# Two-block transformer step on one core: block 1's gate steps and sigmoids a beat further apart, keys' decay ahead of the queries', pooled means in two beats, pooled products in a rotation bank

## The chip, the cores and the metric

One core of a Trainium2 chip runs the whole program. The metric is the device time of one execution in microseconds (us), the median of several; less is better. The engines are TensorE (PE, its weight loads PEld), VectorE (DVE), ScalarE (ACT), GpSimd (POOL) and SyncE (SP). Each runs its own list of instructions in order and waits on semaphores for the others.

## What is computed

512 tokens of 1024 features go through two blocks. Block 1, the one that is changed:

```python
h = rmsnorm(x, pre_norm_g)
q_a, f_a, i_a, g_a, u_b, g_b, q_c, k_c, v_c, g_c, f_c = split(h @ w_in)
# a: 4 heads of 64, gated recurrence
f_gate = lb + (1 - lb) * sigmoid(f_a);  log_f_a = log(max(f_gate, TINY))
k_a = (1 - lb) * sigmoid(-f_a)
o_a = hgrn2_chunkwise(silu(q_a), k_a, i_a, log_f_a)    # S_t = diag(f_t) S_{t-1} + k_t v_t^T, o_t = S_t^T q_t
o_a = rmsnorm(o_a per head) * silu(g_a)
# b: trailing means over 2, 4, 8, 16 tokens minus the token, a small product per group
o_b = (multiscale_pool(u_b) @ pool_w) * pool_scale * silu(g_b)
# c: 8 heads of 64, softmax(q k / 8 + sum of log forget), causal
o_c = forgetting_attention(q_c, k_c, v_c, log_sigmoid(f_c)) * silu(g_c)
x = x + rmsnorm(concat(o_a, o_b, o_c) @ w_out, post_norm_g)
```

Block 2 (window attention with sinks, latent attention, gates, a squared-ReLU feed-forward of width 4096) follows; the change does not touch it.

## The kernel before

Features lie on the 128 partitions and the 512 tokens along the free side. float32 products are made of three float32r products each: the high part of the weights by the high part of the features (L339), the high by the low (L340) and the low by the high (L341). A weight piece of 128x1024 is called a chunk. SyncE loads it, ACT rounds it to its high part (`hi`, L931), DVE subtracts to get the low part (`lo`, L1360), and PE uses it in 24 matmuls, six for each quarter.

Block 1's middle is written out by hand in 80 **beats** (`BEATS1`), and every engine walks through the same beats in one loop; a beat is only a place in each engine's order, not a time. What stands within a beat is done in the order of the code. The table `FILL1` gives each beat one or two quarters of a chunk for PE, so that PE always has large products between the small ones. Around them run:

- **Attention, 16 steps n of 4 beats.** PE: scores at beat 4n (L545), transposes of the weights (`turn`, L556) at 4n+5, product with the values (`weighted`, L572) at 4n+8. DVE: maxima (L1452) at 4n, the division (L1467, L1471) at 4n+3. ACT: exponents (L1090) at 4n. The transposed weights are copied out of their two banks at beat 4n+6, one by ACT (L1100) and one by DVE (L1478); `weighted` at 4n+8 waits for both.
- **Gate steps of the two head pairs p = 0, 1**, counted from the beat in which the chunk with f_a ends (beats 2 and 30): DVE L1616 (`gz`), ACT three functions (`ga1`, L1125 to L1129), DVE two (`gb`, L1621, L1622), ACT two (`ga2`, L1132, L1134), DVE four (`gf`, `gc`, `kh`, L1625 to L1631), ACT two (`ga3`, L1137, L1139), DVE two with the scan (`gs`, `bh`, L1634, L1636).
- **Sigmoid products (silu) of ten tiles** from the table `SILU1`: DVE L1602, L1606 at `start`, ACT three functions (L1177 to L1181) at `start` + 1, DVE the product (L1609) at the end.
- **The recurrence of pair p from beat `REC[p]`** (10 and 40): for eight levels DVE takes differences (L1575), ACT two exponents (L1112, L1113), POOL two products (L1988, L1993), PE a product of 16 small matmuls (L597, beats REC+3 to REC+10), and DVE merges it by a mask (L1564) one beat later. All levels use the banks 6 and 7, so a level waits for the merge of the one before. Then DVE L1643, ACT L1150 (queries' decay) and L1152 (keys' decay), POOL L1997 (queries) and L1999 (keys), PE transposes the keys (L606), makes states (L617), outputs (L629, L633) and head sums (L640).
- **The pooled part**: POOL window sums (L2010), DVE means (L1694, L1697), PE the product (L650) at `POOLED` (beats 51 and 62), ACT its scaling (L1166), which frees its bank.

The banks 2, 4 and 5 are taken in turn by the chunks (`turns`).

Of the kernel before, what the change touches and what calls it, by code (L numbers as in the profile page):

```python
# [82 lines left out]
for c in range(CH["w1e", 0], CH["w1e", 9] + 1):  # L83
    for quarter in range(4):
# [6 lines left out]
SILU1_AT = [END1[CH[SILU1_OF[s][0], SILU1_OF[s][1] * p + SILU1_OF[s][2]]] + 1 for s, p in SILU1]  # L91
SILU1_END = {s: t + 2 for s, t in zip(SILU1, SILU1_AT)}

REC = [max(END1[CH["w1e", 2 * p]] + 7, SILU1_END["q", p]) + 1 for p in range(2)]
POOLED = [next(t for t in range(END1[CH["w1e", 4 + 2 * p]] + 6 + 2 * p, BEATS1)
               if all(t - r < 3 or t - r == 11 or t - r > 17 for r in REC)) for p in range(2)]

# [67 lines left out]
def build(nc, A, out):  # L165
    with ExitStack() as ctx:
# [167 lines left out]
        def pe(e):  # L334
# [306 lines left out]

            def pooled(p):
                bank, before = tenant(6 + p, "pw", p)
                if before:
                    e.wait_ge(*to(*before))
                e.wait_ge(*to("wp", p, 1))
                if p == 0:
                    for g in range(4):
                        e.wait_ge(semaphore(f"pw{g}"), 16)
                e.matmul(bank[:], PWM[:, p, :], WP, start=True, stop=True).then_inc(*up("pm", p))  # L650
# [14 lines left out]
            for t in range(BEATS1):  # L665
# [6 lines left out]
                for p in range(2):  # L672
                    d = t - REC[p]
                    if 3 <= d < 11:
                        level(p, d - 3)
                    if d == 12:
                        keys_by_token(p)
                    if d == 13:
                        states(p)
                    if d == 15:  # L680
                        outputs(p)
                    if d == 16:
                        head_sums(p)
                    if t == POOLED[p]:
                        pooled(p)
                for c, q in FILL1.get(t, ()):
# [238 lines left out]
        def act(e):  # L925
# [177 lines left out]
            for t in range(BEATS1):  # L1103
# [15 lines left out]
                for p in range(2):  # L1119
# [3 lines left out]
                    if d == 2:  # L1123
# [5 lines left out]
                        e.activation(x, x, ACT.Ln, bias=one).then_inc(*up("ga1", p, 2))  # L1129
                    if d == 4:  # L1130
                        e.wait_ge(*to("gb", p, 0))
                        e.activation(BH, BH, ACT.Exp).then_inc(*up("ga2", p, 0))  # L1132
                        e.wait_ge(*to("gb", p, 1))
                        e.activation(KH, x, ACT.Exp, scale=-1.0).then_inc(*up("ga2", p, 1))  # L1134
                    if d == 6:
                        e.wait_ge(*to("gc", p, 0))
# [9 lines left out]

                    d = t - REC[p]
                    if d == 10:
                        e.wait_ge(*to("bh", p))
                        e.activation(QE, BH, ACT.Exp).then_inc(*up("qx", p))  # L1150
                        e.wait_ge(*to("ux", p))
                        e.activation(UR[1], UR[1], ACT.Exp).then_inc(*up("uy", p))  # L1152
                        e.activation(eb, BH[:, 127:T:128], ACT.Exp).then_inc(*up("eb", p))
# [200 lines left out]
        def dve(e):  # L1354
# [184 lines left out]
            for t in range(BEATS1):  # L1539
# [57 lines left out]
                for k, ((s, p), start) in enumerate(zip(SILU1, SILU1_AT)):  # L1597
                    z, o = ZS[k % 2], silu_out(s, p)
                    if t == start:
# [6 lines left out]
                        e.tensor_scalar(o, z, ZMIN, None, ALU.max).then_inc(*up("sm", s, p))  # L1606
                    if t == start + 2:
                        e.wait_ge(*to("sa", s, p, 2))
                        e.tensor_tensor(o, o, z, ALU.mult).then_inc(*up("silu", s, p))  # L1609
                for p in range(2):  # L1610
# [3 lines left out]
                    if d == 1:  # L1614
                        e.wait_ge(*to("gemm", CH["w1e", 2 * p]))
                        e.tensor_tensor(z, seat["gz", p][:], R[:], ALU.mult).then_inc(*up("gz", p))  # L1616
                    if d == 3:
                        if p:
# [3 lines left out]
                        e.scalar_tensor_tensor(x, z, 0.0, x, ALU.max, ALU.add).then_inc(*up("gb", p, 1))  # L1622
                    if d == 5:
                        e.wait_ge(*to("ga2", p, 0))
# [6 lines left out]
                        e.tensor_scalar(KH, KH, oml[:, p:p + 1], None, ALU.mult).then_inc(*up("kh", p))  # L1631
                    if d == 7:
                        e.wait_ge(*to("ga3", p, 1))
# [5 lines left out]
                    d = t - REC[p]  # L1639
                    if d == 10:  # L1640
                        b3, U = (x_.rearrange("p (c s) -> p c s", c=4) for x_ in (BH, UR[1]))
# [43 lines left out]
                    if t == a + 1:  # L1685
                        e.wait_ge(*to("gemm", CH["w1e", 4 + 2 * p]))
                        e.wait_ge(*to("zero", 5))
                        e.tensor_tensor(U[:, 16:528], seat["pu", p][:], R[:], ALU.mult).then_inc(*up("pu", p))
                    if t == a + 4:
                        for b in range(2):  # L1690
                            s = (V, UP2)[b]
# [255 lines left out]
        def pool(e):  # L1947
# [31 lines left out]
            for t in range(BEATS1):  # L1979
                for p in range(2):  # L1980
                    d = t - REC[p]
                    for lv in range(7):
                        if d == (lv if lv > 1 else 0):
# [9 lines left out]
                            e.tensor_tensor(U[:, :, 0:m], U[:, :, 0:m], k[:, :, 0:m],  # L1993
                                            ALU.mult).then_inc(*up("u2", p, lv))
                    if d == 10:
                        e.wait_ge(*to("qx", p))
                        e.tensor_tensor(QE, QE, QH, ALU.mult).then_inc(*up("qe", p))  # L1997
                        e.wait_ge(*to("uy", p))
                        e.tensor_tensor(UR[1], UR[1], KH, ALU.mult).then_inc(*up("ut", p))  # L1999
                    if t == END1[CH["w1e", 4 + 2 * p]] + 1:  # L2000
# [243 lines left out]
```

## Time and profile before

| what | us |
|---|---|
| runs of the kernel before | 1004.94, 1009.93, 1005.14 (median 1005.14) |
| the profiled execution: own time, span | 1009.88, 1008.6 |
| PE busy, PEld busy | 969.3, 790.3 |
| DVE, ACT, POOL busy | 592.7, 425.7, 103.6 |

The span is from the first to the last instruction. A busy PE need not run at its full rate: matmuls overlap, and the clock that the chip grants it is listed apart. In a timeline a row gives the start, the duration, the engine and line, what is written and read, and in brackets how long the engine was idle just before and what ended that. Where the text speaks of a beat's time, it is the start of the first row that belongs to it.

### The profile page before, as it was taken

The numbers are of one execution on the slowest core, as the hardware profiler recorded it, in microseconds if no ns is written. First come the engines' busy times: TensorE is split into PE (matmuls) and PEld (weight loads), VectorE is DVE, ScalarE is ACT, GpSimd is POOL, SyncE is SP. The second block draws the span as 40 slices with busy tenths as digits, with TensorE's granted clock in tenths as the row PEclk, the third lists the DMA queues.
The fourth block names the chain that finished last, engine by engine and source line by source line (L and its number), as shares of the span: only waits on it lengthen the run. The fifth ranks groups of instructions, "written<-read, shape, count | busy, mean of one in ns | idle before, by whom it ended". The sixth has DMA issues, their size and how long they took to land.

```text
span 1008.6 us, 13904 instructions
## 1 busy us (share of the span) xinstructions
PE 969.3 (96%) x5344; PEld 790.3 (78%) x5344; DVE 592.7 (59%) x1104; ACT 425.7 (42%) x816; POOL 103.6 (10%) x110
## 2 busy tenths in 40 slices
PE   9999999999999998999998999999999999999996
PEld 8868777767898775766776889888888888888895
DVE  6467559758748676656655751784235335434456
ACT  6354246345555244645544323463233224213331
POOL 2004103310030000000000312021000000000020
PEclk9999999999999999999999999999999999999999
DMA  7221122112223311212222252253322332332102
GB/s 248 82 83 48 38 64 83 43 42 77 95 92 122 129 42 50 72 30 71 63 63 62 86 188 84 77 215 105 98 91 84 105 97 92 104 105 84 42 1 84
DMA packets 25809, 86.74 MB, mean 86 GB/s; under 512 B 2960, under 2 KB 5712, under 8 KB 25488
## 3 DMA queue, kind: packets, MB, share of 16 engines
q1 hardware_dynamic: 23952, 80.25, 25.0%
q10 hardware_dynamic: 1552, 5.28, 1.4%
q8 instruction: 43, 0.70, 0.3%
q0 software_dynamic: 240, 0.33, 0.1%
q14 instruction: 22, 0.18, 0.1%
HBM read 81.65 MB, written 4.19 MB: 85 GB/s over the span
## 4 chain that ended last, share of the span: by engine, by line
PE 81%; DVE 11%; ACT 5%; issue 3%; POOL 0%; DVEq 0%; ACTq 0%
PE PB L339 11%; PE PB L341 11%; PE PB L340 11%; PE PB L900 5%; PE PB L901 5%; PE PB L899 5%; PE PB L545 3%; PE PB L572 3%; DVE wl L1360 2%; PE PB L556 2%; PE PB L865 1%; PE PB L370 1%; PE PB L867 1%; PE PB L371 1%; PE PB L375 1%
## 5 line engine op out<-in xcount | busy, mean ns | idle before, releaser
L339 PE MATMUL PB<-hh,wh 128*128 128x512 f32 x592 | 248.1, 419 | 3.5 <-DVE AR L1779 1.9
L341 PE MATMUL PB<-hh,wl 128*128 128x512 f32 x592 | 232.5, 393 | 0.0
L340 PE MATMUL PB<-hl,wh 128*128 128x512 f32 x592 | 231.9, 392 | 0.0
L1360 DVE TENSOR_TENSOR wl<-raw,wh 128x1024 fp32r<-128x1024 f32 (+2 forms) x92 | 117.4, 1276 | 65.0 <-ACT wh L931 64.9
L339 PEld LDWEIGHTS PB<-hh,wh 128*128 128x128 f32 x592 | 111.8, 189 | 36.2 <-issue 12.2
L341 PEld LDWEIGHTS PB<-hh,wl 128*128 128x128 f32 x592 | 111.5, 188 | 24.5
L340 PEld LDWEIGHTS PB<-hl,wh 128*128 128x128 f32 x592 | 112.1, 189 | 23.8 <-issue 3.3
L931 ACT ACTIVATE wh<-raw 128x1024 fp32r<-128x1024 f32 (+2 forms) x92 | 93.5, 1019 | 55.8 <-PE PB L867 13.7
L1090 ACT ACTIVATE S<-S,sm 128x256 f32<-128x256 f32 (+3 forms) x96 | 50.8, 530 | 129.0 <-DVE sm L1452 92.2
L1360 DVE TENSOR_TENSOR wl<-AR,wh 128x1024 fp32r<-128x1024 f32 x55 | 67.7, 1231 | 46.0 <-ACT wh L931 46.0
L931 ACT ACTIVATE wh<-AR 128x1024 fp32r<-128x1024 f32 x55 | 57.9, 1052 | 70.3 <-PE PB L901 70.3
L899 PE MATMUL PB<-gh,wh 128*128 128x512 f32 x224 | 87.1, 389 | 0.0
L900 PE MATMUL PB<-gl,wh 128*128 128x512 f32 x224 | 87.1, 389 | 0.0
L901 PE MATMUL PB<-gh,wl 128*128 128x512 f32 x224 | 87.1, 389 | 0.0
L1896 DVE TENSOR_TENSOR tmp<-tmp 128x512 f32<-128x512 f32 x32 | 23.2, 726 | 77.1 <-ACT gh L1306 77.1
L1302 ACT ACTIVATE tmp<-PB 128x512 f32<-128x512 f32 x32 | 19.1, 596 | 90.0 <-PE PB L341 87.8
L1452 DVE CUSTOM_DVE_ANT_0 S<-PB,MK 128x128 f32<-128x128 f32 (+3 forms) x64 | 29.9, 490 | 37.9 <-PE PB L545 37.1
L899 PEld LDWEIGHTS PB<-gh,wh 128*128 128x128 f32 x224 | 42.0, 188 | 8.8
L900 PEld LDWEIGHTS PB<-gl,wh 128*128 128x128 f32 x224 | 42.0, 188 | 8.7
L901 PEld LDWEIGHTS PB<-gh,wl 128*128 128x128 f32 x224 | 42.0, 188 | 8.7
L1961 POOL TENSOR_TENSOR acc<-acc,tmp 128x512 f32<-128x512 f32 x11 | 15.9, 1450 | 315.2 <-ACT tmp L1330 284.6
L572 PE MATMUL PB<-PT,AR 128*64 128x128 f32 x432 | 34.7, 286 | 11.2 <-ACT PT L1100 5.7
(356 smaller groups left out, 1722.5 us busy)
## 6 DMA issues: line engine op xcount, KB each, us to landing
AR<-in_dne SPq DMA_DIRECT2D x32, 512.0 KB, 3.5
AR<-in_upe SPq DMA_DIRECT2D x24, 512.0 KB, 3.5
raw<-in_w2g SPq DMA_DIRECT2D x16, 512.0 KB, 3.5
raw<-in_w1e SPq DMA_DIRECT2D x10, 512.0 KB, 3.5
raw<-in_w1q SPq DMA_DIRECT2D x8, 512.0 KB, 3.4
raw<-in_woab SPq DMA_DIRECT2D x8, 512.0 KB, 3.5
raw<-in_w2e SPq DMA_DIRECT2D x6, 512.0 KB, 4.1
X<-in_xT SPq DMA_DIRECT2D x4, 512.0 KB, 6.4
```

The costliest lines, as they stand in the source:

```text
L339: e.matmul(bank[:], a[:, col(k)], xa[:, k, :], start=k == 0, stop=False)
L340: e.matmul(bank[:], a[:, col(k)], xb[:, k, :], start=False, stop=False)
L341: i = e.matmul(bank[:], b[:, col(k)], xa[:, k, :], start=False, stop=k == 7)
L545: last = e.matmul(bank[b][:, k], query[b], key[b][:, k], start=a == 2, stop=x == parts - 1)
L572: x = e.matmul(bank[rows(b), col(i)], v, PT[b][:, j - lo, :], start=j == lo, stop=j == i)
L899: e.matmul(bank[:], a[:, col(k)], gh[:, k, :], start=k == 0, stop=False)
L900: e.matmul(bank[:], a[:, col(k)], gl[:, k, :], start=False, stop=False)
L901: i = e.matmul(bank[:], b[:, col(k)], gh[:, k, :], start=False, stop=k == 7)
L931: e.activation(wide_high if c == LAST else wh[c % 3][:, 0:PLAN[c][2]], raw_of(c), ACT.Copy).then_inc(*up("hi", c))
L1090: e.activation(s, s, ACT.Exp, bias=nm, scale=-1.0, accum_out=su).then_inc(*up("exp", a, n, b))
L1360: e.tensor_tensor(low_, raw_of(c), high.bitcast(F32), ALU.subtract).then_inc(*up("lo", c))
L1452: e.tensor_tensor_reduce(soft(n, b)[:, 0:w], seat["max", a, n, b][:, 0:w], MK[:, T - w:T], -1.0, BIG, ALU.add, ALU.min, scalars(n, b)[0]). ...
```

## The change

Six tables and places are edited:

- A silu takes 3 beats instead of 2 from its start to the DVE product; the ACT part stays in beat `start` + 1.
- Gate steps, in beats after the chunk's end: `gb` 3 to 4, `ga2` 4 to 5, `gf`/`gc`/`kh` 5 to 7, `ga3` 6 to 8, `gs`/`bh` 7 to 10. `gz` and `ga1` stay at 1 and 2.
- `REC` goes from (10, 40) to (13, 41).
- L1643 and the keys' decay (ACT L1152, POOL L1999) go to REC + 9, the queries' stay at REC + 10. They were all at REC + 10, queries first.
- The second half of each pooled mean goes one beat later.
- `POOLED` stays (51, 62), by a shorter rule; its product takes the next of the banks 2, 4, 5 instead of bank 6 or 7.

```diff
-SILU1_END = {s: t + 2 for s, t in zip(SILU1, SILU1_AT)}
-
-REC = [max(END1[CH["w1e", 2 * p]] + 7, SILU1_END["q", p]) + 1 for p in range(2)]
-POOLED = [next(t for t in range(END1[CH["w1e", 4 + 2 * p]] + 6 + 2 * p, BEATS1)
-               if all(t - r < 3 or t - r == 11 or t - r > 17 for r in REC)) for p in range(2)]
+SILU1_END = {s: t + 3 for s, t in zip(SILU1, SILU1_AT)}
+
+REC = [max(END1[CH["w1e", 2 * p]] + 10, SILU1_END["q", p]) + 1 for p in range(2)]
+POOLED = [END1[CH["w1e", 4 + 2 * p]] + 6 + 2 * p for p in range(2)]
...
-            def pooled(p):
-                bank, before = tenant(6 + p, "pw", p)
-                if before:
-                    e.wait_ge(*to(*before))
+            def pooled(p, at):
+                bank, before = tenant(at, "pw", p)
+                e.wait_ge(*to(*before))
...
-                        pooled(p)
+                        pooled(p, (2, 4, 5)[turns % 3])
+                        turns += 1
...
-                    if d == 4:
+                    if d == 5:
                         e.wait_ge(*to("gb", p, 0))
...
-                    if d == 6:
+                    if d == 8:
                         e.wait_ge(*to("gc", p, 0))
...
                     d = t - REC[p]
+                    if d == 9:
+                        e.wait_ge(*to("ux", p))
+                        e.activation(UR[1], UR[1], ACT.Exp).then_inc(*up("uy", p))
                     if d == 10:
                         e.wait_ge(*to("bh", p))
                         e.activation(QE, BH, ACT.Exp).then_inc(*up("qx", p))
-                        e.wait_ge(*to("ux", p))
-                        e.activation(UR[1], UR[1], ACT.Exp).then_inc(*up("uy", p))
...
-                    if t == start + 2:
+                    if t == start + 3:
                         e.wait_ge(*to("sa", s, p, 2))
...
-                    if d == 3:
+                    if d == 4:
                         if p:
                             e.wait_ge(*to("ho", 0))
...
-                    if d == 5:
+                    if d == 7:
                         e.wait_ge(*to("ga2", p, 0))
...
-                    if d == 7:
+                    if d == 10:
                         e.wait_ge(*to("ga3", p, 1))
...
-                    if d == 10:
+                    if d == 9:
                         b3, U = (x_.rearrange("p (c s) -> p c s", c=4) for x_ in (BH, UR[1]))
...
-                    if t == a + 4:
-                        for b in range(2):
+                    for b in range(2):
+                        if t == a + 4 + b:
...
+                    if d == 9:
+                        e.wait_ge(*to("uy", p))
+                        e.tensor_tensor(UR[1], UR[1], KH, ALU.mult).then_inc(*up("ut", p))
                     if d == 10:
                         e.wait_ge(*to("qx", p))
                         e.tensor_tensor(QE, QE, QH, ALU.mult).then_inc(*up("qe", p))
-                        e.wait_ge(*to("uy", p))
-                        e.tensor_tensor(UR[1], UR[1], KH, ALU.mult).then_inc(*up("ut", p))
```

VectorE, the first pair's gate, beats 5 to 6, before (L1621 and L1622 are `gb`, L1360 the low part of a chunk, L1478 a softmax copy, L1602 and L1606 the start of a silu):

```order
L1621 SCALAR_TENSOR_TENSOR AR<-early 128x512
L1622 SCALAR_TENSOR_TENSOR early<-early 128x512
L1360 TENSOR_TENSOR wl<-raw,wh 128x1024
L1478 COPY PT<-PB 128x128
L1602 TENSOR_TENSOR tmp<-PB,R 128x512
L1606 TENSOR_SCALAR AR<-tmp 128x512
```

and in the changed kernel:

```order
L1360 TENSOR_TENSOR wl<-raw,wh 128x1024
L1478 COPY PT<-PB 128x128
L1602 TENSOR_TENSOR tmp<-PB,R 128x512
L1606 TENSOR_SCALAR AR<-tmp 128x512
L1621 SCALAR_TENSOR_TENSOR AR<-early 128x512
L1622 SCALAR_TENSOR_TENSOR early<-early 128x512
```

The two steps `gb` stand behind four others now. Pair 1 has the same exchange in beats 33 and 34.

VectorE, the second pair, beats 33 to 35, before (L1467 and L1471 divide the softmax, L1625 to L1631 are `gf`, `gc` and `kh`):

```order
L1621 SCALAR_TENSOR_TENSOR AR<-early 128x512
L1622 SCALAR_TENSOR_TENSOR early<-early 128x512
L1360 TENSOR_TENSOR wl<-raw,wh 128x1024
L1478 COPY PT<-PB 128x512
L1602 TENSOR_TENSOR tmp<-PB,R 128x512
L1606 TENSOR_SCALAR AR<-tmp 128x512
L1467 RECIPROCAL sm<-sm 128x2
L1471 TENSOR_SCALAR S<-S,sm 128x128 x2
L1625 TENSOR_SCALAR AR<-AR,sm 128x512
L1628 TENSOR_SCALAR early<-AR 128x512
L1630 TENSOR_SCALAR early<-AR 128x512
L1631 TENSOR_SCALAR AR<-AR,sm 128x512
```

and where L1625 to L1631 stand in the changed kernel, beats 36 and 37 (L1452 are the maxima, L1609 a silu's product):

```order
L1452 ISA S,sm<-PB,MK 128x256
L1452 ISA sm 128x1
L1452 ISA S,sm<-PB,MK 128x256
L1452 ISA sm 128x1
L1360 TENSOR_TENSOR wl<-raw,wh 128x1024
L1609 TENSOR_TENSOR AR<-AR,tmp 128x512
L1602 TENSOR_TENSOR tmp<-PB,R 128x512
L1606 TENSOR_SCALAR AR<-tmp 128x512
L1625 TENSOR_SCALAR AR<-AR,sm 128x512
L1628 TENSOR_SCALAR early<-AR 128x512
L1630 TENSOR_SCALAR early<-AR 128x512
L1631 TENSOR_SCALAR AR<-AR,sm 128x512
```

The four steps went from ahead of the maxima to behind the maxima, the next chunk's low part and two pieces of silu.

ScalarE, beats 36 to 38, before (L1137 and L1139 are `ga3`, L1031 rounds an attention output, L1177 to L1181 a silu, L1100 the softmax copy of step 8):

```order
L1090 ACTIVATE S,sm<-S,sm 128x256 x2
L931 ACTIVATE wh<-raw 128x1024
L1137 ACTIVATE early<-early 128x512
L1139 ACTIVATE early<-early 128x512
L1031 ACTIVATE gh<-tmp 128x512
L1177 ACTIVATE AR<-AR 128x512
L1179 ACTIVATE AR<-AR,con 128x512
L1181 ACTIVATE AR<-AR 128x512
L1100 ACTIVATE PT<-PB 128x128
```

and in the changed kernel, where these lines have numbers that are one lower:

```order
L1089 ACTIVATE S,sm<-S,sm 128x256 x2
L930 ACTIVATE wh<-raw 128x1024
L1136 ACTIVATE early<-early 128x512
L1138 ACTIVATE early<-early 128x512
L1177 ACTIVATE AR<-AR 128x512
L1179 ACTIVATE AR<-AR,con 128x512
L1181 ACTIVATE AR<-AR 128x512
L1030 ACTIVATE gh<-tmp 128x512
L1099 ACTIVATE PT<-PB 128x128
```

On this engine only the rounding of the attention output moved here; the same instructions stand ahead of the softmax copy.

## Rows read from the trace of the kernel before

**Rows 1.** The page: busy time of PE, and the chain that ended last by engine

```profile
PE 969.3 (96%) x5344; PEld 790.3 (78%) x5344; DVE 592.7 (59%) x1104; ACT 425.7 (42%) x816; POOL 103.6 (10%) x110
...
PE 81%; DVE 11%; ACT 5%; issue 3%; POOL 0%; DVEq 0%; ACTq 0%
```

**Rows 2.** Waits of PE, 51 to 252 us: total, times, longest

```profile
PE PB L597 <- DVE AR L1564: 3.6, 3, 2.3
PE PB L572 <- ACT PT L1100: 2.3, 1, 2.3
PE PB L606 <- ACT early L1166: 2.2, 1, 2.2
PE PB L606 <- POOL AR L1999: 1.9, 1, 1.9
PE PB L572 <- DVE PT L1478: 0.7, 1, 0.7
```

**Rows 3.** Busy time by 5 us stretches; behind "PEclk" is the granted clock

```profile
75.00:80.00 5.00, 4.54 (x23) 3.17 (x24) 3.30 (x6) 2.37 (x6) 3.96 (x6) 0.66 0.01 3
115.00:120.00 5.00, 5.00 (x27) 3.64 (x27) 2.63 (x8) 0.00 (x0) 0.00 (x0) 0.66 0.04 16
195.00:200.00 5.00, 2.72 (x21) 2.14 (x20) 4.36 (x9) 1.41 (x4) 0.73 (x1) 0.82 0.15 56
200.00:205.00 5.00, 5.00 (x18) 3.72 (x17) 1.64 (x5) 2.63 (x4) 0.55 (x1) 0.84 0.00 0
```

**Rows 4.** Timeline of PE: beats 12 and 40, and the keys' transposes of pair 1

```profile
75.47 1.12 PE L572 MATMUL PB<-PT,AR 128*64 128x128 f32 x8 [2.34 <-ACT PT L1100]
...
161.41 0.44 PE L572 MATMUL PB<-PT,AR 128*64 128x128 f32 x4
...
209.45 0.55 PE L606 MATMUL PB<-con,AR 128*128 128x128 f32 x3 [2.22 <-ACT early L1166]
```

**Rows 5.** Timeline of ACT ahead of beat 12

```profile
60.38 1.04 ACT L931 ACTIVATE wh<-raw 128x1024 fp32r<-128x1024 f32 x1
...
73.81 0.42 ACT L1112 ACTIVATE AR<-AR 128x256 f32<-128x256 f32 x1 [3.43 <-DVE AR L1575]
...
75.05 0.36 ACT L1100 ACTIVATE PT<-PB 128x256 f32<-128x256 f32 x1
```

**Rows 6.** Timeline of DVE, beats 33 to 38

```profile
147.75 0.69 DVE L1621 SCALAR_TENSOR_TENSOR AR<-early 128x512 f32<-128x512 f32 x1 [2.75 <-ACT early L1129]
...
148.96 1.22 DVE L1360 TENSOR_TENSOR wl<-raw,wh 128x1024 fp32r<-128x1024 f32 x1
...
151.76 0.16 DVE L1467 RECIPROCAL sm<-sm 128x2 f32<-128x2 f32 x1
...
152.35 0.54 DVE L1625 TENSOR_SCALAR AR<-AR,sm 128x512 f32<-128x512 f32 x1
...
156.72 1.23 DVE L1360 TENSOR_TENSOR wl<-raw,wh 128x1024 fp32r<-128x1024 f32 x1 [0.37 <-ACT wh L931]
157.87 0.68 DVE L1602 TENSOR_TENSOR tmp<-PB,R 128x512 f32<-128x512 f32 x1
...
158.93 0.68 DVE L1634 TENSOR_TENSOR early<-early 128x512 f32<-128x512 f32 x1
```

**Rows 7.** Timeline of ACT, beats 33 to 38

```profile
147.56 1.04 ACT L931 ACTIVATE wh<-raw 128x1024 fp32r<-128x1024 f32 x1
...
155.65 1.04 ACT L931 ACTIVATE wh<-raw 128x1024 fp32r<-128x1024 f32 x1
156.60 0.61 ACT L1137 ACTIVATE early<-early 128x512 f32<-128x512 f32 x1
...
157.64 0.61 ACT L1031 ACTIVATE gh<-tmp 128x512 fp32r<-128x512 f32 x1
159.05 0.64 ACT L1177 ACTIVATE AR<-AR 128x512 f32<-128x512 f32 x1 [0.80 <-DVE AR L1606]
...
161.01 0.26 ACT L1100 ACTIVATE PT<-PB 128x128 f32<-128x128 f32 x1
```

## The prediction

> **What bounds the kernel now.** I read the page first: PE is busy for 969.3 us of 1008.6, and the chain that ended last is PE for 81% [rows 1]. No other engine is near that, so only two things can be won: stretches in which PE stands idle, and stretches in which it runs below its full clock. The change touches block 1 alone, which lies between 51 and 252 us. The waits of PE there sum up to 10.7 us in seven places [rows 2]. In order of time they are: 2.34 us at beat 12 (the first L572 behind the softmax copy of step 1 [rows 4]), 0.80 before a level, 1.89 before the keys' transposes of pair 0, 0.52 and 2.28 before levels of pair 1, 2.22 before pair 1's keys' transposes [rows 4], and 0.69 before L572 at beat 60. The clock view adds a second price. It shows four stretches of 5 us below 1.00: 0.66, 0.66, 0.82 and 0.84 [rows 3]. They are three falls to the lower of the two levels, 1.2 instead of 2.4 GHz, and stand behind the waits of 2.34, 1.89 and 2.28 us. Each loses 5 x 0.34 = 1.7 us (the third 5 x 0.18 + 5 x 0.16 = 1.7), 5.1 us in all. The wait of 2.22 us had no such fall behind it. So block 1 holds 15.8 us that can be won in the profiled execution.
>
> The profiled execution took 1009.88 us, the median of the three runs is 1005.14, and one run took 1009.93. The difference of 4.7 is about the 5.1 us of the three falls. I take 1005.1 to be an execution without them, which no row proves. Half a per cent, 5 us, is about what a measurement of this kernel can tell from no change.
>
> **What the change removes.** Wait by wait:
> - The keys' transposes of pair 0 waited for POOL L1999, which stood behind the queries' L1997 in the beat just before. Now the keys' product starts three beats ahead of the transposes. Between them PE has two levels and some 24 large matmuls, an estimate of over 6 us, and the chain is one instruction each of DVE, ACT and POOL (L1643, L1152, L1999), so the 1.89 us go. The queries' product is needed three beats after the keys', so turning the two round costs nothing.
> - The transposes of pair 1 waited 2.22 us for L1166, since the pooled product sat in their bank 6. In a rotation bank it blocks the third chunk after it, six or more beats later. The 2.22 us go. Pooled product 1 shifts the last chunk to bank 5, which the output projection wants seventh; DVE L1602 frees it about then, which costs 0.1 us at most.
> - The 2.28 us before a level of pair 1 waited for a merge (L1564) behind both halves of the pooled mean, four instructions of together 1.9 us. Half of these now stand a beat later, still a beat ahead of the pooled product that reads them, and the levels stand a beat later too. By the sum of DVE's instructions in the two beats the merge is ready when PE comes. The 0.52 and 0.80 us before levels go likewise: the levels of pair 0 begin three beats after the gates, not beside them.
> - The 0.69 us at beat 60 go, because the head norm now comes behind that copy.
> - Beat 12 keeps most of its wait. The softmax copy stood behind pair 0's exponents [rows 5]; these move to beat 13, but the gate steps come closer. I lay the durations out from L931's end at 61.42 [rows 5]: low part, copy and silu start take 2.4 us on DVE, `gb` 1.3 (65.1); ACT does `ga2`, three sigmoid steps, exponents and the next high part until 69.9; DVE follows with low part, two products and four gate steps, 4.0 us, and ACT ends `ga3` and the copy at 74.7. PE could start at 74.8 instead of 75.47 [rows 4], so 0.67 us are won.
> That is 0.80 + 1.89 + 0.52 + 2.28 + 2.22 + 0.69 + 0.67 = 9.1 us of idle time.
>
> **What the change adds.** The same thing happens to pair 1, where before there was no wait: PE took L572 of beat 40 at 161.41 without one [rows 4], ACT's copy having begun at 161.01 [rows 7]. Laid out step by step:
> 1. `gb` stands behind the low part. DVE must now wait for L931, which ends at 147.56 + 1.04 = 148.60 [rows 7]. Low part, copy, L1602 and L1606 took 151.76 - 148.96 = 2.8 us [rows 6], so `gb` runs from 151.4 to 152.7 instead of 147.75 to 149.0 [rows 6].
> 2. ACT: `ga2` until 153.3, three sigmoid steps 2.0, two exponents 1.0, high part 1.04, until 157.3 (before 156.69 [rows 7]).
> 3. DVE: low part 1.15 (156.72 to 157.87 [rows 6]), L1609 0.6, L1602 and L1606 1.06 (157.87 to 158.93 [rows 6]), then L1625 and L1628 1.0. `gc` is ready at 161.1. Before, L1625 began at 152.35 [rows 6] and ACT could start `ga3` at 156.60 [rows 7].
> 4. ACT: `ga3` 1.1, three sigmoid steps and the copy 2.2 (159.05 to 161.27 [rows 7]), the rounding L1031 0.5: the copy ends at 165.0. PE wanted it at 161.41.
> This makes a wait of 3.6 us. Pair 0's head norm, now in beats 29 and 30, pushes `gz` by an estimated 0.9 us more (its four dependent DVE steps stand ahead of the division and of `gz`), so the bounds are 3.6 and 4.5 and I take 4.1. Queued behind that copy are ACT's next high part and exponents, and behind PE's L572 all of PE.
> Next late is pair 1's scan at beat 40, then the first exponents and the copy for beat 44: 0.85 us if PE runs at full clock, nothing if it is slowed. Beat 16 has the like for pair 0, 0.55 or nothing. Pair 1's states at beat 54 wait for a DVE copy that now stands behind L1712 and a silu product: 1.0 us. Together 5.1 us if PE is slowed, 6.5 if not. The later silu products cost nothing by themselves: their readers (the attention output L1712, the levels, the pooled and recurrent outputs) were put at or behind the new beat, and PE's large products of that beat cover them. No DMA is moved: SyncE's queue is as before, and its loads follow the low parts, whose place among the beats is the same; the one low part that is later, by 0.6 us in step 3, is read three beats on.
>
> **The clock.** The three falls of before go with their waits, but new waits stay at beats 12 (1.7 us) and 40 (4.1 us), and I take both to have a fall behind them, 3.4 us. The bounds are none and six. *The Trainium skill* ("TensorE: Matmul & The Clock Gate", Part 1) has the gate look at activity at times that do not follow the kernel's start, so that the same kernel can fall in one run and not in another. By that rule the runs of before at 1005 and 1010 would differ in this alone, and the change would move the slower kind more than the faster. The trace has a wait of 2.28 us with a fall and one of 2.22 without [rows 2, 3], which fits it; the sum does not need it.
>
> **The sum.** Against the profiled execution: 1009.9 - 9.1 + 5.1 - 5.1 + 3.4 = 1004.2. Against 1005.1 taken as free of falls: 1005.1 - 9.1 + 5.1 + 3.4 = 1004.5, or without any fall 1005.1 - 9.1 + 6.5 = 1002.5. I predict 1004.0.
>
> **The rivals.**
> - *The knot at beat 38 is not there.* If `gc` is ready before ACT comes to it, ACT's copy is in time and 4.1 + 1.7 us fall away: 998.2. For it: the instructions ahead of the copy are the same as before. Against it: `gc` is ready 7.8 us later by the sums above (161.1 against 152.35 + 1.0 [rows 6]); before, even the last gate step L1634 had begun by 158.93 [rows 6].
> - *Waits only move.* DVE is what PE waits for behind both levels [rows 2], so each us won before a level might come back one beat later. All in all no time is won: 1005.1. For it: the 0.80 and 0.52 us. Against it: the two waits at the transposes have other causes.
> - *Slower: the clock falls behind the small waits too.* At full clock the new waits are 6.5 us, which gives 1002.5. Each fall adds 1.7. From five falls on, behind the waits at beats 12, 16, 40, 44 and 54, it is 1011.0, slower than before by over half a per cent; four make 1009.3. For it: 1.89 us sufficed once. Against it: the waits of 0.52 to 0.80 us had no fall, nor had the one of 2.22 us [rows 2, 3].
>
> **How the numbers follow.** The forecast has a chance of 0.50, the absent knot 0.22, the moved waits 0.16, the clock 0.12. Faster by over half a per cent (below 1000.1): 0.22 and a tail of 0.05 of the forecast's, 0.27. Slower (above 1010.2): 0.12. Within: 0.61. The range goes from 998.5, next to the absent knot, to 1009.5, just short of the fifth fall.
>
> **What would show it.** In the trace after, PE waits at beat 40 for ACT's copy (L1099) for 3.6 to 4.5 us, and ACT ahead of it for `gc` (L1136 behind DVE's L1628). PE waits 1.7 us at beat 12 for a copy. Neither transposes (L605) nor levels (L596) have waits over 0.5 us. A wait at beat 40 under 1 us, or a new one over 2 us elsewhere in block 1, would make the prediction wrong, as would falls of the clock that do not follow waits.

## The result and the profile after

The kernel before took 1006.63 us (median of five runs, 1004.94 to 1009.93), the changed one 1014.71 (five runs, 1014.05 to 1015.71). The ratio is 1.0074 with a 95% interval of [1.0047, 1.01]: slower by 0.74%. (Here and below the ratio is worked out from all runs; it is not the quotient of the two medians.) Predicted were 1004.0 us and a range of 998.5 to 1009.5.

The profiled execution of the changed kernel took 1014.05 us. Its page, which answers to [rows 1]:

```profile
span 1012.8 us, 13904 instructions
...
PE 969.6 (96%) x5344; PEld 791.4 (78%) x5344; DVE 592.9 (59%) x1104; ACT 425.0 (42%) x816; POOL 104.4 (10%) x110
...
PE 75%; DVE 13%; ACT 7%; issue 3%; POOL 0%; DVEq 0%; ACTq 0%
```

PE is as busy as before, within 0.3 us, in a span that is 4.2 us longer: the time went into idleness of PE. In the chain that ended last, PE has 75% instead of 81%. The waits of PE in block 1 (51 to 252 us), as in [rows 2]. Most line numbers are one lower than before: L571 is `weighted`, L596 a level, L616 the states, L1099 the ACT copy.

```profile
PE PB L571 <- ACT PT L1099: 6.7, 4, 4.1
PE PB L596 <- POOL AR L1988: 2.2, 1, 2.2
PE PB L616 <- issue: 1.3, 1, 1.3
PE PB L596 <- DVE AR L1564: 1.1, 2, 0.8
...
```

The same view of 252 to 290 us, behind the beats. In the kernel before it has no row at all.

```profile
PE PB L338 <- DVE wl L1360: 2.3, 1, 2.3
PE PB L369 <- DVE tmp L1602: 0.7, 1, 0.7
```

The two stretches sum up to 14.5 us of idle time (before: 10.7). In the timeline of PE the four that matter most are:

```profile
91.20 1.11 PE L596 MATMUL PB<-AR 64*128 64x64 f32 x16 [2.17 <-POOL AR L1988]
...
163.57 0.44 PE L571 MATMUL PB<-PT,AR 128*64 128x128 f32 x4 [4.10 <-ACT PT L1099]
...
252.01 0.50 PE L369 MATMUL PB<-gh,wh 128*128 128x512 f32 x1 [0.67 <-DVE tmp L1602]
...
275.06 0.50 PE L338 MATMUL PB<-gh,wh 128*128 128x512 f32 x1 [2.33 <-DVE wl L1360]
```

The granted clock in stretches of 5 us, the answer to [rows 3] (the third number from the end):

```profile
90.00:95.00 5.00, 3.80 (x29) 3.76 (x30) 3.10 (x10) 4.94 (x13) 2.71 (x4) 0.74 0.01 3
95.00:100.00 5.00, 5.00 (x47) 4.76 (x46) 3.73 (x6) 1.96 (x5) 3.06 (x3) 0.92 0.30 105
160.00:165.00 5.00, 1.43 (x12) 1.29 (x14) 2.58 (x8) 4.35 (x8) 0.00 (x0) 0.91 0.03 8
165.00:170.00 5.00, 5.00 (x21) 3.82 (x18) 4.13 (x9) 1.31 (x4) 0.00 (x0) 0.75 0.17 47
...
550.00:555.00 5.00, 5.00 (x27) 4.12 (x28) 1.40 (x2) 2.18 (x3) 0.00 (x0) 0.68 0.01 3
```

Three falls, each of about 1.7 us (5 x 0.26 + 5 x 0.08, and so on): behind the waits of 2.17 and 4.10 us, and one in block 2, where the change moves nothing.

### The profile page after: what moved, and what is told of

Same layout as the page of the kernel before. It is cut to its first block, busy times and chain, and to the rows that moved or that the text cites. A ratio compares the mean times of both kernels' runs of the same rounds, so it can differ in the third digit from the quotient of the medians.

```text
span 1012.8 us, 13904 instructions
## 1 busy us (share of the span) xinstructions
PE 969.6 (96%) x5344; PEld 791.4 (78%) x5344; DVE 592.9 (59%) x1104; ACT 425.0 (42%) x816; POOL 104.4 (10%) x110
## 4 chain that ended last, share of the span: by engine, by line
PE 75%; DVE 13%; ACT 7%; issue 3%; POOL 0%; DVEq 0%; ACTq 0%
PE PB L338 10%; PE PB L340 10%; PE PB L339 10%; PE PB L900 5%; PE PB L899 5%; PE PB L898 5%; PE PB L544 3%; DVE wl L1360 3%; PE PB L571 3%; ACT wh L930 2%; PE PB L864 1%; ACT S L1089 1%; PE PB L865 1%; PE PB L866 1%; PE PB L555 1%
## 5 line engine op out<-in xcount | busy, mean ns | idle before, releaser
L1360 DVE TENSOR_TENSOR wl<-raw,wh 128x1024 fp32r<-128x1024 f32 (+2 forms) x92 | 117.7, 1280 | 84.0 <-ACT wh L930 83.8
L338 PEld LDWEIGHTS PB<-hh,wh 128*128 128x128 f32 x592 | 111.5, 188 | 35.8 <-issue 11.7
L1360 DVE TENSOR_TENSOR wl<-AR,wh 128x1024 fp32r<-128x1024 f32 x55 | 67.7, 1231 | 46.0 <-ACT wh L930 46.0
L1452 DVE CUSTOM_DVE_ANT_0 S<-PB,MK 128x128 f32<-128x128 f32 (+3 forms) x64 | 29.9, 489 | 33.9 <-PE PB L544 33.1
L571 PE MATMUL PB<-PT,AR 128*64 128x128 f32 x432 | 35.1, 289 | 14.9 <-ACT PT L1099 10.1
L571 PEld LDWEIGHTS PB<-PT,AR 128*64 128x64 f32 x432 | 23.5, 139 | 32.1 <-issue 18.6
```

The source lines that it names most:

```text
L338: e.matmul(bank[:], a[:, col(k)], xa[:, k, :], start=k == 0, stop=False)
L571: x = e.matmul(bank[rows(b), col(i)], v, PT[b][:, j - lo, :], start=j == lo, stop=j == i)
L1360: e.tensor_tensor(low_, raw_of(c), high.bitcast(F32), ALU.subtract).then_inc(*up("lo", c))
L1452: e.tensor_tensor_reduce(soft(n, b)[:, 0:w], seat["max", a, n, b][:, 0:w], MK[:, T - w:T], -1.0, BIG, ALU.add, ALU.min, scalars(n, b)[0]). ...
```

## One reading for all runs

Each run lists its span and its mean granted clock. A run's time multiplied by that clock is what it would have taken without the falls; I call it the clock-free time. Runs of one kernel that lie up to 8 us apart agree in it within 3 us (the clock is listed to 0.001, which is 1 us). It comes out some 2.4 to 2.8 us too low for every kernel, since the clock also falls over about the last 5 us of the program, when PE has nothing to do (granted clock 0.50 from 1004 us on before, from 1008 us on after). Beside it stands what the profile shows as PE's waits from 51 to 290 us, summed up. The medians and ratios are those of the runs below, each beside runs of the kernel before in the same round; "rest" is clock-free time less waits.

| kernel | runs | median us | ratio to before | clock-free us | waits us | rest |
|---|---|---|---|---|---|---|
| before | 5 to 35 | 1006.6 to 1009.6 | | 1002.0 | 10.7 | 991.3 |
| after | 5 | 1014.71 | 1.0074 [1.0047, 1.01] | 1005.6 | 14.5 | 991.1 |
| e8, after again | 6 | 1016.18 | 1.0068 [1.0044, 1.0091] | 1005.5 | 14.5 | 991.0 |
| e1, `ga` silu back | 12 | 1010.04 | 1.0018 [1.0001, 1.0034] | 1003.4 | 11.2 | 992.2 |
| e2, pair 1's gates back | 12 | 1009.38 | 1.0007 [0.9991, 1.0022] | 1003.5 | 11.7 | 991.8 |
| e9, all silus back | 12 | 1008.09 | 0.9993 [0.9972, 1.0014] | 999.6 | 8.6 | 991.0 |
| e3, bank alone | 12 | 1011.76 | 1.0013 [0.999, 1.0036] | 1000.6 | 9.5 | 991.1 |
| e4, keys alone | 12 | 1006.32 | 0.9983 [0.9965, 1.0] | 1000.2 | 9.0 | 991.2 |
| e5, means alone | 12 | 1008.61 | 1.0006 [0.9989, 1.0024] | 1000.9 | 9.6 | 991.3 |
| e6, silus alone | 11 | 1011.95 | 1.0042 [1.0025, 1.0059] | 1004.1 | 12.3 | 991.8 |
| e7, bank, keys, means | 12 | 1004.51 | 0.9965 [0.9949, 0.9981] | 998.4 | 7.5 | 990.9 |
| e10, e7 and `REC` 11, 40 | 6 | 1002.63 | 0.9934 [0.9912, 0.9955] | 996.7 | 5.8 | 990.9 |
| e11, e10 and an early copy | 6 | 999.10 | 0.9898 [0.9876, 0.9919] | 995.5 | 4.0 | 991.5 |

The rest is 990.9 to 992.2 for all of them, while the waits go from 4.0 to 14.5. So, within about 1 us, a microsecond in which PE waits here costs a microsecond, and what is left of a difference between medians is the clock. Nothing is given back later: behind 290 us PE's waits sum up to 17.3 us before and 17.2 after, in the same places. For the changed kernel: 3.8 us more of waits, and a median 9.1 us above its clock-free time where before's first five runs stood 4.6 above theirs.

## The experiments

The expectations reckon from 1006.6 us, the first five runs of the kernel before. In the rounds of the experiments the same kernel had medians of 1009.54 (e1 to e4), 1009.64 (e5 to e7) and 1008.06 (e8 to e11), so their absolute times are up to 3 us low from the start. What decides is the wait that each expects, and the clock-free time.

**e1: is the tail the `ga` silus?** The sigmoid products of `ga`, the last of which falls behind the beats' end, go back to `start` + 2.

```diff
-SILU1_END = {s: t + 3 for s, t in zip(SILU1, SILU1_AT)}
+SILU1_END = {s: t + (2 if s[0] == "ga" else 3) for s, t in zip(SILU1, SILU1_AT)}
...
-                    if t == start + 3:
+                    if t == SILU1_END[s, p]:
```

> The changed kernel with the two last silu tiles (ga, pairs 0 and 1) back at their old distance of 2 beats. Tail theory: the loss behind the beats comes from the DVE products and roundings of these tiles, which push the angle chain and with it the low part for which the output projection waits (2.33 us, and 0.7 for bank 5); the wait before the fifth chunk of the projection goes, the time falls by about 3 us from 1014.7 to 1011.6. Knot theory (the loss is in the waits at beats 12, 16, 17 and 40): no change, 1014.7 within 0.5. Clock theory (the loss is how often the clock falls): the wait goes, but the time moves by whole falls of 1.7 us in either direction.

Measured: median 1010.04. Between 252 and 290 us the waits are gone, and the rows of the tail stand where they stood in the kernel before, to 0.01 us:

```profile
258.23 0.42 DVE L1722 CAST S<-AR 128x512 f32<-128x512 int32 x1
...
270.95 1.22 DVE L1360 TENSOR_TENSOR wl<-raw,wh 128x1024 fp32r<-128x1024 f32 x1 [4.10 <-ACT wh L930]
```

It follows that 3.0 us of waits came from these two entries of the table. The wait of 4.10 stayed (4.12). PE's waits fell by 3.3 us in all, the clock-free time by only 2.2; about 1 us between this kernel's waits and its time is not accounted for.

**e2: is the knot at beat 40 the gates?** Pair 1's gate steps go back to their old offsets, pair 0's stay.

```diff
-                    if d == 5:
+                    if d == (5, 4)[p]:
...
-                    if d == 8:
+                    if d == (8, 6)[p]:
...
-                    if d == 4:
+                    if d == (4, 3)[p]:
...
-                    if d == 7:
+                    if d == (7, 5)[p]:
...
-                    if d == 10:
+                    if d == (10, 7)[p]:
```

> The changed kernel with the gate steps of pair 1 alone back at their old offsets (REC of pair 1 stays 41). Knot theory: the wait of 4.1 us at beat 40 goes and with it a fall of the clock, 1014.7 - 4.1 - 1.7 = 1008.9. Tail theory: the tail is not touched, its 3 us stay, so 1009 is also the floor here. If the wait at beat 40 were made by the shifted attention output or by pair 0's head norm instead, at least 3 us of it would stay and the time would be above 1012.

Measured: 1009.38. Of the 4.10 us, 1.91 remained, so pair 1's gates are 2.2 of them and not the whole; it was expected to go. The tail kept its 0.67 and 2.33, as it should.

**e3: the rotation bank alone**, on the kernel before.

```diff
-                        pooled(p)
+                        pooled(p, (2, 4, 5)[turns % 3])
+                        turns += 1
```

> The kernel before with only the pooled products in the rotation banks. The wait of 2.22 us before pair 1's key transposes goes; nothing else moves: 1006.6 - 2.2 = 1004.4. Rival: the last chunk of the beats now sits in bank 5 and the output projection waits for it (0.7 to 1.1 us), which leaves 1005.3 or so. If waits only move, 1006.6.

Measured: 1011.76, ratio 1.0013. The wait of 2.22 us is gone, but the states L617 (L616 after) come with 1.7 us that were not there. PE reaches them sooner, and the copy of the transposed keys on DVE (L1649), queued behind a low part and the start of a silu, is not ready (e11 tests this). The 0.69 us at beat 60 went too, so the net gain is 1.2 us (10.7 to 9.5). Bank 5 made no wait. That this kernel's median is no better is the clock: seven of its twelve runs lie at 1011.7 to 1013.6 with a mean clock of 0.987 or 0.989, the other five at 1005.3 to 1007.5 with 0.994 or 0.996.

**e4 and e5: the keys' decay alone, the means alone**, on the kernel before.

```diff
-                    if d == 10:
+                    if d == 9:
                         b3, U = (x_.rearrange("p (c s) -> p c s", c=4) for x_ in (BH, UR[1]))
```

```diff
-                    if t == a + 4:
-                        for b in range(2):
+                    for b in range(2):
+                        if t == a + 4 + b:
```

(In e4 the keys' exponent on ACT and their product on POOL go to 9 with it, as in the change.)

> The kernel before with only the keys' decay a beat earlier and ahead of the queries'. The wait of 1.89 us before pair 0's key transposes goes, and the fall of the clock behind it: 1006.6 - 1.9 - 1.7 = 1003.0; without the fall 1004.7. Rival: the DVE difference and the ACT exponent now come before ACT's copy of the softmax in that stretch and one of these is late: 1006.6 or more.

> The kernel before with only the second half of each pooled mean a beat later. The four DVE instructions ahead of the merge that PE waits for (2.28 us in the trace before, beat 50) become two; the merge is about 1 us earlier if its beat holds the second half behind it: the wait shrinks to 1.3 us or less, and the clock may not fall: 1006.6 - 1.0 = 1005.6, with the fall 1003.9. If waits only move: 1006.6.

Measured: 1006.32 and 1008.61. In e4 the wait of 1.89 us for POOL is gone and a level waits 0.2 longer, so 1.7 is won. In e5 the level's 2.28 shrinks to 1.17: the mean was half of it. For the rest, the rows show DVE at other work in those beats; no run tried it.

**e6: the silus alone**, on the kernel before. Since pair 1's queries end a beat later, `REC` becomes (10, 41).

```diff
-SILU1_END = {s: t + 2 for s, t in zip(SILU1, SILU1_AT)}
+SILU1_END = {s: t + 3 for s, t in zip(SILU1, SILU1_AT)}
...
-                    if t == start + 2:
+                    if t == start + 3:
```

> The kernel before with only the silu products a beat later (this moves REC of pair 1 to 41 too, since its query silu ends later). Tail theory: the low part for the projection is 2.85 us later here too and PE waits for it about 2.3 us: 1006.6 + 2.3 = 1008.9 or more. Knot theory: no wait over 1 us appears at the tail, 1006.6.

Measured: 1011.95, slower than before by 0.42%, from this edit and the one beat of `REC` that comes with it. PE's waits, with the tail's:

```profile
PE PB L572 <- ACT PT L1100: 4.4, 2, 2.9
PE PB L597 <- DVE AR L1564: 2.7, 2, 1.9
...
PE PB L339 <- DVE wl L1360: 2.7, 1, 2.7
```

The first row counts two waits. The second of them is 1.50 us at beat 40, where before had none: the silus begin the knot with the old gates. In the rows there, ACT's rounding of the attention output (L1031) waits 0.39 us for its DVE product (L1712), which now stands behind the scan, and the softmax copy stands behind that rounding. The last row is the tail.

**e9: the silus back**, on the changed kernel: the reverse of e6's edit. `REC` stays (13, 41).

> The changed kernel with all silu products back at 2 beats; gates, REC (13, 41) and the three moves as changed. Tail theory: the whole tail wait (2.33 and 0.7) goes. Knot theory as put in the prediction (the gate steps alone make the wait at beat 40): about 3.5 us of the 4.1 stay, floor 1009.0 - 3.1 - 0.5 = 1005.4. If silu and gates make that wait together, 2 us or less of it stay: floor 1003.8 or less.

Measured: 1008.09, ratio 0.9993. No wait behind 252 us, and in block 1:

```profile
PE PB L571 <- ACT PT L1099: 4.7, 3, 3.0
PE PB L596 <- POOL AR L1988: 2.2, 1, 2.2
...
```

The gates without the silus make 3.0 us at beat 40, the silus without the gates 1.5, both 4.1. Neither expectation (3.5 stays, or 2 and less) was met; the two share the wait. The clock-free time fell from 1005.6 to 999.6.

**e7: the three moves without gates and silus**: e3, e4 and e5 together, on the kernel before.

> The kernel before with the three moves that cost nothing in the trace after: rotation bank, keys' decay first, pooled mean in two beats. Gates, silu and REC as before. If the single gains add up: 2.2 + 1.9 + 1.0 of waits and up to two falls of 1.7: 1006.6 - 5.1 - 3.4 = 998.1; without the falls 1001.5. If waits only move, 1005 or more.

Measured: 1004.51, ratio 0.9965 [0.9949, 0.9981], the first kernel that is faster. Its waits:

```profile
PE PB L597 <- DVE AR L1565: 2.8, 3, 1.4
PE PB L572 <- ACT PT L1100: 2.3, 1, 2.3
PE PB L617 <- issue: 1.7, 1, 1.7
...
```

**e8: the changed kernel again**, beside e9 to e11.

> The changed kernel, unchanged, beside the others. Floor theory: a run takes a floor that is fixed by the waits, plus 1.4 to 1.7 us for every fall of the clock. The floor of this kernel is 1014.05 - 5.1 = 1009.0 by its trace, that of before 1009.9 - 5.1 = 1004.8; the runs should lie on 1009.0, 1010.6, 1012.2, 1013.9, 1015.5 and before on 1004.8 to 1012.5 in the same steps. Rival: the spread is noise without steps, and the ratio stays at 1.0074.

Measured: 1016.18, ratio 1.0068 [1.0044, 1.0091], with the same waits. The profiled execution took 1017.50 and had five falls: those of the three places above, one at 275 behind the tail's 2.33, and one at 345 to 355 in block 2. Of the expected ladder (1009.0, 1010.6, 1012.2, 1013.9, 1015.5) the lower half was not seen: all eleven runs of this kernel, in both rounds, lie between 1014.05 and 1017.5, so a changed kernel without falls is worked out and not measured.

**e10 and e11: on from e7.** e10 puts pair 0's recurrence one beat later, beside the old gates; e11 also moves DVE's copy of the transposed keys ahead of the low part of its beat (and takes it out of its old place, which the cut leaves out).

```diff
-REC = [max(END1[CH["w1e", 2 * p]] + 7, SILU1_END["q", p]) + 1 for p in range(2)]
+REC = [max(END1[CH["w1e", 2 * p]] + 8 - p, SILU1_END["q", p]) + 1 for p in range(2)]
```

```diff
+                for p in range(2):
+                    d = t - REC[p]
+                    if d == 12:
+                        e.wait_ge(*to("kp", p))
+                        if p:
+                            e.wait_ge(*to("sg", 0))
+                        e.tensor_copy(KT, seat["kt", p][:, 0:384].rearrange("p (c s) -> p c s", c=3)).then_inc(
+                            *up("kt", p))
                 for c, end in END1.items():
                     if t == end + 1:
                         lo(c + 2)
```

> The three moves (rotation bank, keys first, mean in two beats) on the kernel before, with the recurrence of pair 0 one beat later (REC 11 instead of 10), gates and silu as before. The softmax copies of step 1 then stand ahead of pair 0's first differences and exponents on DVE and ACT: the wait at beat 12 shrinks from 2.34 to 0.5 us and no clock fall follows. Floor 1000.2 - 1.8 = 998.4. If waits only move, the levels of pair 0 wait instead and the floor stays at 1000.2.

> As the run before, and the DVE copy of the transposed keys stands ahead of the low part and the silu steps of its beat. The wait of pair 1's states (1.7 us with the three moves) was put down to nothing in the profile; if it is this copy, it goes and the floor falls by 1.2 to 1.7 us more. If it is something else, the time does not change.

Measured: 1002.63 and 999.10. In e10 the 2.34 us at beat 12 shrink to 0.40 with one beat for `REC[0]` and no gate step moved. In e11 the 1.7 us ahead of the states are gone too. What is left of PE's waits in block 1 in e11:

```profile
PE PB L597 <- DVE AR L1565: 3.1, 3, 1.4
PE PB L572 <- DVE PT L1479: 0.9, 2, 0.5
```

e11 is faster than before by 1.0% (0.9898 [0.9876, 0.9919]) and its median is 17 us below that of the changed kernel in the same round (e8). From e10 to e11 the waits fell by 1.8 us and the clock-free time by 1.2; the rest of the 3.5 us between the medians is the clock.

## Why the prediction was wrong, by its own steps

**The knot at beat 40 was right in its chain, and met its number in part by luck.** Predicted was a wait of 3.6 to 4.5 us for ACT's copy with `gc` (L1628) late ahead of it, taken at 4.1. The timeline of ACT and DVE there (compare [rows 6, 7]):

```profile
155.86 1.23 DVE L1360 TENSOR_TENSOR wl<-raw,wh 128x1024 fp32r<-128x1024 f32 x1 [2.91 <-ACT wh L930]
157.00 0.68 DVE L1609 TENSOR_TENSOR AR<-AR,tmp 128x512 f32<-128x512 f32 x1
...
158.67 0.54 DVE L1625 TENSOR_SCALAR AR<-AR,sm 128x512 f32<-128x512 f32 x1
159.24 0.43 DVE L1628 TENSOR_SCALAR early<-AR 128x512 f32<-128x512 f32 x1
...
159.71 0.63 ACT L1136 ACTIVATE early<-early 128x512 f32<-128x512 f32 x1 [3.88 <-DVE early L1628]
...
162.70 0.61 ACT L1030 ACTIVATE gh<-tmp 128x512 fp32r<-128x512 f32 x1
163.22 0.26 ACT L1099 ACTIVATE PT<-PB 128x128 f32<-128x128 f32 x1
```

ACT sits 3.88 us until `gc` is there, does `ga3`, three sigmoid steps and a rounding, and comes to the copy at 163.22; PE starts at 163.57. The copy ends 1.5 us earlier than in the prediction (163.5 against 165.0), and PE wants it 1.9 us earlier (159.47 against 161.41). The two misses nearly cancel, and a wait of 4.10 is the 3.6 of the sum with that difference, not with the head norm's 0.9 that the prediction had added by estimate. Of its parts the rounding L1030 and the product L1609 (0.5 and 0.6 us) come from the silus: without them it was 3.0 (e9).

**So were the small ones.** Beat 12: 1.66 us (predicted 1.7). Beat 16: 0.64 (0.55 or 0). Beat 44: 0.33 (0.85 or 0). States at beat 54: 1.26 (1.0). The waits at the transposes and those of 0.52 and 0.69 us went, as said. Block 1's last beat ended 0.9 us earlier than before, in spite of 0.7 us more idle time within it: one fall fewer lay there.

**Failed: "The later silu products cost nothing by themselves."** The step looked at who reads the products and at PE's work in the beats, and the prediction took its waits from 51 to 252 us alone, as "the change touches block 1 alone". It did not lay out what the products do to DVE's and ACT's queues in the last beats and behind them, where DVE and ACT already work out the sines for the next block's positions (the angle chain, L1722 to L1738). The timeline after:

```profile
250.67 0.68 DVE L1609 TENSOR_TENSOR early<-early,tmp 128x512 f32<-128x512 f32 x1
...
253.06 0.63 ACT L1030 ACTIVATE gh<-AR 128x512 fp32r<-128x512 f32 x1 [3.56 <-DVE AR L1678]
253.59 0.62 ACT L1177 ACTIVATE early<-early 128x512 f32<-128x512 f32 x1
...
256.18 0.69 DVE L1435 TENSOR_TENSOR gl<-tmp,gh 128x512 fp32r<-128x512 f32 x1 [1.77 <-ACT gh L1030]
256.79 0.68 DVE L1609 TENSOR_TENSOR early<-early,tmp 128x512 f32<-128x512 f32 x1
...
259.92 1.23 DVE L1360 TENSOR_TENSOR wl<-raw,wh 128x1024 fp32r<-128x1024 f32 x1 [0.26 <-ACT wh L930]
261.06 0.42 DVE L1722 CAST S<-AR 128x512 f32<-128x512 int32 x1
...
269.72 0.63 ACT L1194 ACTIVATE AR<-S 128x512 f32<-128x512 f32 x1 [7.59 <-DVE S L1738]
...
273.78 1.23 DVE L1360 TENSOR_TENSOR wl<-raw,wh 128x1024 fp32r<-128x1024 f32 x1 [4.09 <-ACT wh L930]
```

And the same instructions before:

```profile
248.14 0.68 DVE L1609 TENSOR_TENSOR early<-early,tmp 128x512 f32<-128x512 f32 x1
...
249.65 0.63 ACT L1031 ACTIVATE gh<-AR 128x512 fp32r<-128x512 f32 x1 [0.37 <-DVE AR L1678]
...
251.85 0.63 ACT L1177 ACTIVATE early<-early 128x512 f32<-128x512 f32 x1 [1.57 <-DVE early L1606]
...
253.94 0.69 DVE L1609 TENSOR_TENSOR early<-early,tmp 128x512 f32<-128x512 f32 x1 [0.92 <-ACT early L1181]
...
257.07 1.23 DVE L1360 TENSOR_TENSOR wl<-raw,wh 128x1024 fp32r<-128x1024 f32 x1 [0.25 <-ACT wh L931]
258.22 0.42 DVE L1722 CAST S<-AR 128x512 f32<-128x512 int32 x1
...
266.88 0.63 ACT L1194 ACTIVATE AR<-S 128x512 f32<-128x512 f32 x1 [7.58 <-DVE S L1738]
...
270.94 1.23 DVE L1360 TENSOR_TENSOR wl<-raw,wh 128x1024 fp32r<-128x1024 f32 x1 [4.10 <-ACT wh L931]
...
272.49 0.39 PE L339 MATMUL PB<-gh,wh 128*128 128x512 f32 x1
```

The delay is made in two places. First, pair 0's `ga` product (L1609) stands behind a low part and not ahead of it, at 250.67 instead of 248.14. The rounding of its norm product on ACT comes at 253.06 instead of 249.65, and pair 1's sigmoid steps are queued behind that rounding: they begin 1.74 us later. Second, pair 1's product stands behind the low part of the attention output (L1435), which itself waits 1.77 us for ACT; that makes another 1.11. Together the last silu product is 2.85 us later, and everything behind it 2.84: the next low part, the angle chain (L1722), ACT's function at its end (L1194), the high part that ACT has queued behind it, and the low part that PE needs. Before, that low part was ready at 272.17 and PE came for it at 272.49, so 0.32 us were to spare, and no row shows a wait; the view of waits gave no hint of it. Shown by e1, e9 (gone) and e6 (there again, 2.7 us, without the other edits). The two places are read from the rows; no run moved one of them alone.

The same step failed a second time at beat 40: e6 has 1.50 us there from the silus, and of the 4.10 they make 1.1 (e9 against the changed kernel).

"Costs 0.1 us at most", for bank 5 freed by L1602, is the 0.67 us at 252.01: L1602 stands behind a silu product there (L1609). It takes both: it went with e1 (bank, no late `ga` product), e3 (bank, no late silu) has none, and e6 (late silus, old banks) has none for L1602 either.

**Failed: the levels.** The prediction had the 2.28 us go and 0.80 and 0.52 "go likewise". Three levels still wait, 2.17 + 0.30 + 0.81 (the last where the 2.28 was), and the first is over the 2 us that I had set as the mark of a wrong prediction. For the one at 91.20 the profile names POOL's L1988. The level that starts there is the second; its product on POOL was ready at 87.5, and the L1988 named works for a later level. What it needs and what ended last is the merge of the level before it in the same banks (L1564, 90.29 to 91.05):

```profile
86.11 1.65 DVE L1471 TENSOR_SCALAR S<-S,sm 128x512 f32<-128x512 f32 x2
87.68 0.68 DVE L1602 TENSOR_TENSOR tmp<-PB,R 128x512 f32<-128x512 f32 x1
...
88.73 1.22 DVE L1575 TENSOR_TENSOR AR<-AR 128x512 f32<-128x512 f32 x1
...
90.29 0.76 DVE L1564 COPY_PREDICATED AR<-msk,PB 128x256 f32<-128x256 uint8 x2
```

DVE is busy without a gap from 84.77 to 91.05. `REC` at 13 set the first levels beside attention's step 3 and the start of a silu; with `REC` at 11 and the old gates (e10) pair 0's levels wait 1.11 us at most. The silu products have no part in it: without them the wait is 2.2 all the same (e9). That it is this crowding I read from the rows; no run moved only one of these instructions.

**Mis-sized: the clock.** The term was 3.4 us, two falls. The median run of the changed kernel has 1014.7 - 1005.6 - 2.7 (the end) = 6.4. The clock followed waits less neatly than the prediction supposed: in the changed kernel there was no fall behind the 1.66 us of beat 12, and one in block 2. The same wait of 2.33 us at beat 12 has a fall behind it in before, e4 and e7 and none in e3 and e5.

**The sum again with what was measured.** Predicted idle time was 10.7 - 9.1 + 5.1 = 6.7 us, found are 14.5: 7.8 more, of which 3.0 the tail, 3.3 the levels, 1.0 the waits at beats 16 and 44 that were taken as nothing, 0.5 small ones. The clock adds 3.0. 1004.0 + 7.8 + 3.0 = 1014.8, against 1014.71. That this closes to 0.1 us is luck in part, since 1004.0 itself was chosen between sums of 1002.5, 1004.2 and 1004.5. Of the rivals, "slower" had the right side for a part of the right reason (more falls), and "waits only move" had the levels; the tail was in none of them.

**What the parts are worth,** by clock-free times: bank, keys and means -3.6 (e7), the gates and `REC` on top of them +1.2 (e9), the silus on top of both +6.0. The silus alone cost 2.1 net (e6). They make nearly the same new waits in both, 5.4 us in e6 and 5.8 in the changed kernel (against e9). But in e6 3.8 us of old waits went at the same time (2.22, 0.69, 0.52 and 0.36 of the 2.28), with the beat of `REC[1]` that comes with the silus; in the changed kernel these had gone already. No run moved `REC[1]` alone.

## What to carry to other kernels

A delay by one slot in a table must be followed to the end of the section and behind it, in the queues of the engines that do the moved work: a low part with no wait in the profile may have been in time by less than the delay (here by 0.32 us, against 2.84). Price each part of a bundled change alone; here three good moves worth 3.6 us hid behind two that cost 7.2, and the wait at beat 12, of which the bundle took 0.7 us, needed only one later beat of `REC[0]` (2.34 to 0.40). Where times of one kernel are scattered, compare run time times granted clock, and check it against the sum of the waits.

## What the runs showed of the hardware that was not expected

The same kernel's times lie in steps. The 35 runs of before beside e1 to e4, all on one chip, stand near 1004.9, 1006.5, 1007.9, 1009.7, 1011.1 and 1012.5, with mean clocks from 0.998 down to 0.989. I read each step of 1.4 to 1.8 us as one more fall, from none to five; the one execution that was traced (1009.88 us) has three, which fits. The median of that unchanged kernel was 1006.63 in one round and 1009.54 in another, nearly as much as the three moves gain. The Trainium skill ("TensorE: Matmul & The Clock Gate", Part 1) says that the gate's looks do not follow the kernel's start; these runs agree, as their times and mean clocks differ for the same instructions. Ten of the thirteen profiles have a fall between 535 and 560 us, in block 2, where no edit moves anything, and three have none there. Why the kernel with the bank alone fell to 0.987 in five of its runs is open; no run tried it.

A second thing stands in the rows ahead of the late merge. The same form of difference (L1575, 128x512) took 1.22 us at 88.73, between products of POOL, and 0.68 at 92.98. That the two engines slow each other is what the rows suggest. It was not measured alone, and the two rows belong to different levels, whose access differs.
